# State injection of an S5 layer with the tokens as the stationary operand, and moved modulation panels

## The chip, the cores and the metric

The kernel runs on one core of a Trainium2 chip. The metric is the device time of one execution in microseconds (us). Before: 2250.16 us, the median of three runs (2249.39 to 2253.13).

## The reference, cut to what matters

Four layers on 256 latent and 256 context tokens of 1024 channels: attention, Hyena, S5, FNet, each followed by a SwiGLU feed-forward (FFN). The change lies in the S5 mixer (layer 2), in the join ahead of it and in the one ahead of FNet (layer 3). S5 computes, for both directions, a linear recurrence over the context tokens and then over the latent ones:

```
bu = einsum('bngc,gsc->bngs', u, b_bar)        # the injection: 64 groups of 16 channels, 64 complex states each
xs = associative_scan(_lin_rec, (lam_bar, bu), reverse=reverse)
xs_lat = xs_lat + a_cum * h0                    # the context's last state carried into the latent tokens
y_lat = y_lat + einsum('bngs,gcs->bngc', xs_lat, c_mat).real
out = a * sigmoid(b), a, b = split(gelu(y_lat) @ w_glu + b_glu)
```

At FNet: `f = fftn(hg, axes=(1, 3)).real`, then a projection; the transform over channels comes first.

## The kernel before, in words

Every engine runs its own hand-written list of work, stage by stage, and semaphores order them. The program's classes are stages: `Join` (the norm, residual and modulation between two sub-layers), `S5`, `Ffn`, `Fnet`. Eight steps of tokens form a chunk, so a direction has 32 context and 32 latent chunks of 8 tokens; the scan runs over chunks, the inside of a chunk is done by a Toeplitz product.

**S5 on TensorE** (`S5.tensor`). The injection runs 16 rounds of four groups. Each round has eight matmuls (L2470) with a 128 x 128 block of weights `et` as the stationary operand and 64 columns of tokens `u` (32 latent and 32 context chunks) as the moving one; their sum lies in bank 0 or 1 with the states on the partitions, forward states on partitions 0 to 63, backward ones on 64 to 127. In the trace an ordinary f32 matmul stands as two MATMUL records, a transpose as one. After round 7 TensorE takes the "turn" of one modulation unit (L374). Then come 64 Toeplitz matmuls (L2484), two modulation panels ("states", L397), the first half of the output products (L2497), four panels ("scan"), the second half, the transposes of y (L2508) with two panels ("turns") between, and the gated projection `up` (L864).

**ScalarE** (`S5.scalar`) moves each round's bank to `e` with three copies (helper line L2516), which put the states in the order of the scan: `e` is (group, real or imaginary, step q in a block of 8 chunks, block b), context ahead of latent blocks, backward rows reversed. **VectorE** (`S5.vector`) first lays out tables (until L2361), waits for `e_moved` and scans: `inside` (L2370 to L2373, seven steps of four operations), `across` (L2380 to L2383), for groups 0 to 15, 16 to 31, then 32 to 63, and at last `carries` (L2425 to L2428) of the second half. GpSimd does the `carries` of the first half once `across` of it is done. ScalarE and VectorE then copy the states to `s2` for the output products.

**SyncE** issues the DMAs in one written order: `et` blocks 0 to 3, the power table, two modulation panels, half of the `u` tokens (GpSimd issues the other half), two modulation panels, eight Toeplitz blocks `m0`, `et` blocks 4 to 7 as slots come free, the output weights `f` in two halves, then modulation panels and the weights of `up`. `f` lies over `et` and `m0`.

**Modulation** (`Modulations`). The 24 vectors that modulate the layers are products with 96 panels of 1 MB. `place(key, n, before)` gives n panels to a slot of TensorE's order and says when SyncE may refetch the two ring buffers. Four panels make a unit; ScalarE copies a finished unit (L408), TensorE turns it (L374), VectorE adds the bias (L418 and the next two). In `Join.tensor` part 0 stands ahead of the spreads (L495), part 1 behind them. `build` gives the join ahead of S5 (2, 2) panels and the join ahead of FNet (2, 0). That last one has a turn in part 1 and nothing else. By this count panels 82 and 83 are part 1 ahead of S5, 84 and 85 "states", 86 to 89 "scan", 90 and 91 "turns".

**FNet** (`Fnet.tensor`): 16 matmuls over channels (L2590), copied by VectorE (L2609), then 32 over tokens (L2599), then the projection (L819). L2590 needs only the channel blocks of h that it reads, which ScalarE writes one by one (L693).

## Time and profile before

| | us |
|---|---|
| median of three runs | 2250.16 |
| the profiled execution | 2252.99 |
| its span in the profile | 2251.2 |
| TensorE busy | 2106.3 (94%) |
| VectorE busy | 1167.2 (52%) |
| ScalarE busy | 865.4 (38%) |
| GpSimd busy | 156.0 (7%) |

Busy is the time in which an engine had an instruction under way; a TensorE that is busy need not stream columns at its full rate. PEclk is the granted clock of TensorE as a share of 2.4 GHz: 1.00 is 2.4 and 0.50 is 1.2 GHz. Idle time is followed by what ended it. "Bank" is PSUM, "arena", "ring" and "tail" are areas of SBUF. Times in rows are us from the start of the span.

### The profile page before, as it was taken

The numbers are of one execution on the slowest core, as the hardware profiler recorded it, in microseconds if no ns is written. First come the engines' busy times: TensorE is split into PE (matmuls) and PEld (weight loads), VectorE is DVE, ScalarE is ACT, GpSimd is POOL, SyncE is SP. The second block draws the span as 40 slices with busy tenths as digits, with TensorE's granted clock in tenths as the row PEclk, the third lists the DMA queues.
The fourth block names the chain that finished last, engine by engine and source line by source line (L and its number), as shares of the span: only waits on it lengthen the run. The fifth ranks groups of instructions, "written<-read, shape, count | busy, mean of one in ns | idle before, by whom it ended". The sixth has DMA issues, their size and how long they took to land.

```text
span 2251.2 us, 31615 instructions
## 1 busy us (share of the span) xinstructions
PE 2106.3 (94%) x13233; PEld 1650.2 (73%) x13233; DVE 1167.2 (52%) x1961; ACT 865.4 (38%) x1416; POOL 156.0 (7%) x213
## 2 busy tenths in 40 slices
PE   4999999999999989988999999997959899898998
PEld 2756557777777767754558888884948899778997
DVE  2322652655566566636254665765571645526454
ACT  2442224533333453220243334245632544525444
POOL 0000000102001100010001200111110000000000
PEclk8999999999999999999999999998579999999998
DMA  6334341645435546442143433444584555314553
GB/s 255 131 124 168 131 149 38 197 146 169 175 133 190 174 150 226 165 144 75 38 150 120 129 117 115 136 138 159 206 337 138 181 187 187 125 57 150 188 180 102
DMA packets 227243, 342.14 MB, mean 152 GB/s; under 512 B 9590, under 2 KB 190625, under 8 KB 224860
## 3 DMA queue, kind: packets, MB, share of 16 engines
q1 hardware_dynamic: 216064, 310.27, 40.2%
q0 software_dynamic: 10320, 29.58, 4.5%
q8 instruction: 105, 1.72, 0.3%
q10 hardware_dynamic: 716, 0.26, 0.0%
q14 instruction: 38, 0.31, 0.0%
HBM read 317.66 MB, written 24.51 MB: 152 GB/s over the span
## 4 chain that ended last, share of the span: by engine, by line
PE 86%; DVE 7%; DMA 3%; ACT 2%; issue 1%; SPq 0%; POOL 0%; ACTq 0%; DVEq 0%
PE bank L953 20%; PE bank L954 20%; PE bank L955 20%; PE bank L819 4%; PE bank L397 4%; PE bank L864 2%; PE bank L2470 2%; PE bank L1719 1%; DMA mod_ring<-mod_w 1%; PE bank L1348 1%; PE bank L637 1%; DMA arena<-mod_w 1%; PE bank L2052 1%; PE bank L627 1%; PE bank L495 1%; PE bank L1673 1%
## 5 line engine op out<-in xcount | busy, mean ns | idle before, releaser
L953 PE MATMUL bank<-h_hi,w_hi 128*128 128x512 f32 (+1 forms) x1480 | 512.4, 346 | 11.1 <-DVE h_lo L725 10.6
L954 PE MATMUL bank<-h_lo,w_hi 128*128 128x512 f32 (+1 forms) x1480 | 505.0, 341 | 0.0
L955 PE MATMUL bank<-h_hi,w_lo 128*128 128x512 f32 (+1 forms) x1480 | 505.0, 341 | 0.0
L915 DVE TENSOR_TENSOR w_lo<-ring,w_hi 128x1024 fp32r<-128x1024 f32 (+1 forms) x282 | 323.8, 1185 | 285.0 <-ACT w_hi L910 284.9
L953 PEld LDWEIGHTS bank<-h_hi,w_hi 128*128 128x128 f32 x1480 | 283.6, 192 | 49.5 <-DVE h_lo L725 13.3
L910 ACT ACTIVATE w_hi<-ring 128x1024 fp32r<-128x1024 f32 (+1 forms) x282 | 274.0, 1019 | 103.8 <-PE bank L955 100.8
L955 PEld LDWEIGHTS bank<-h_hi,w_lo 128*128 128x128 f32 x1480 | 283.4, 191 | 32.1 <-issue 0.2
L954 PEld LDWEIGHTS bank<-h_lo,w_hi 128*128 128x128 f32 x1480 | 283.8, 192 | 29.3 <-issue 0.2
L953 PE MATMUL bank<-g_hi,w_hi 128*128 128x512 f32 (+1 forms) x704 | 241.1, 342 | 0.0
L954 PE MATMUL bank<-g_lo,w_hi 128*128 128x512 f32 (+1 forms) x704 | 236.9, 337 | 0.0
L955 PE MATMUL bank<-g_hi,w_lo 128*128 128x512 f32 (+1 forms) x704 | 236.7, 336 | 0.0
L953 PEld LDWEIGHTS bank<-g_hi,w_hi 128*128 128x128 f32 x704 | 133.5, 190 | 22.6 <-issue 8.7
L955 PEld LDWEIGHTS bank<-g_hi,w_lo 128*128 128x128 f32 x704 | 133.5, 190 | 14.3
L954 PEld LDWEIGHTS bank<-g_lo,w_hi 128*128 128x128 f32 x704 | 133.6, 190 | 12.9
L1073 ACT ACTIVATE g_hi<-arena 128x512 fp32r<-128x512 f32 (+1 forms) x88 | 45.9, 525 | 234.6 <-DVE arena L1098 234.6
L397 PE MATMUL bank<-mod_ring,silu_c 128*32 128x256 f32 x1408 | 98.6, 406 | 24.6 <-DMA mod_ring<-mod_w 24.6
L1067 ACT ACTIVATE arena<-bank 128x512 f32<-128x512 f32 (+1 forms) x88 | 42.7, 490 | 189.4 <-PE bank L955 187.8
L1098 DVE TENSOR_TENSOR arena<-arena,bank 128x512 f32<-128x512 f32 (+1 forms) x88 | 48.2, 551 | 112.6 <-PE bank L955 110.6
L397 PEld LDWEIGHTS bank<-mod_ring,silu_c 128*32 128x32 f32 x1408 | 40.4, 114 | 66.5 <-DMA mod_ring<-mod_w 31.1
L953 PE MATMUL bank<-h_hi,hy_w_hi 128*128 128x512 f32 x192 | 76.5, 398 | 0.7 <-DVE h_lo L725 0.7
L954 PE MATMUL bank<-h_lo,hy_w_hi 128*128 128x512 f32 x192 | 74.9, 390 | 0.0
L955 PE MATMUL bank<-h_hi,hy_w_lo 128*128 128x512 f32 x192 | 74.8, 390 | 0.0
(328 smaller groups left out, 2978.3 us busy)
## 6 DMA issues: line engine op xcount, KB each, us to landing
ring<-ffn_w SPq DMA_DIRECT2D x120, 1024.0 KB, 5.1
mod_ring<-mod_w SPq DMA_DIRECT2D x88, 1024.0 KB, 6.8
ring<-ffn_w SPq DMA_DIRECT2D x16, 768.0 KB, 4.6
ring<-hy_w_in SPq DMA_DIRECT2D x12, 1024.0 KB, 5.2
arena<-mod_w SPq DMA_DIRECT2D x8, 1024.0 KB, 17.1
s_in_weights<-arena POOLq DMA_DIRECT2D x32, 256.0 KB, 3.2
s_out_weights<-arena POOLq DMA_DIRECT2D x16, 512.0 KB, 3.6
arena<-s_in_weights SPq DMA_DIRECT2D x8, 1024.0 KB, 10.8
```

The costliest lines, as they stand in the source:

```text
L397: last = nc.tensor.matmul(MODB[32 * g:32 * g + 32, 0:256], silu_c[:, k, :], self.slot(m)[:, kk, 256 * g:256 * g + 256], start=(k == 0), st ...
L819: last = nc.tensor.matmul(self.banks[c % 4][:, 0:self.n], v[:, kl, q * P:(q + 1) * P], self.rhs(k), start=(k == 0), stop=(k == self.kk - 1))
L864: last = nc.tensor.matmul(self.bank(c, t)[:, 0:self.n], v[:, k, q * P:(q + 1) * P], self.rhs(k), start=(k == 0), stop=(k == KD - 1))
L910: nc.scalar.activation(self.hi[:, i % SPLIT, a:b], self.w.slot(i)[:, a:b], ACT.Copy).then_inc(w_rounded, 1)
L915: unit.tensor_tensor(self.lo[:, i % SPLIT, a:b], self.w.slot(i)[:, a:b], self.hi[:, i % SPLIT, a:b].bitcast(F32), ALU.subtract).then_inc(w ...
L953: nc.tensor.matmul(o, w[0], v[0], start=first, stop=False)
L954: nc.tensor.matmul(o, w[0], v[1], start=False, stop=False)
L955: return nc.tensor.matmul(o, w[1], v[0], start=False, stop=last)
L1067: nc.scalar.activation(self.silus[:, q, 0:n], self.out(i, q)[:, 0:n], ACT.Silu).then_inc(ffn_silu, 1)
L1073: nc.scalar.activation(g_hi[:, c + q, 0:n], self.silus[:, q, 0:n], ACT.Copy).then_inc(ffn_g_rounded, 1)
L1098: nc.vector.tensor_tensor(self.silus[:, q, 0:n], self.silus[:, q, 0:n], self.out(i, q)[:, 0:n], ALU.mult).then_inc(ffn_product, 1)
L2470: last = nc.tensor.matmul(bank[self.INJECT[n % 2]][:, o:o + 2 * CH], self.et[:, c % 4, 4 * (n % 2) + gb, i, :], self.u[:, 4 * n + gb, :], ...
```

## The change

The injection swaps its operands. In each round the 64 token columns of a group are the stationary operand and the 256 weights (128 real, 128 imaginary states) the moving one; four matmuls write bank 0 or 1, two groups side by side on partitions 0 to 63 and 64 to 127, tokens on the partitions (`inject`). The bank is copied to `rows` in SBUF, by VectorE for rounds 0 to 3 and by ScalarE for 4 to 15 (`move_injected`). Eight small products then bring the states back to the partitions (`turn_states`): four transposes for the forward states, four matmuls with the identity read backwards within each 32 columns for the backward ones. They write bank 4 or 5 directly in the order of `e`, in steps of eight elements, and ScalarE copies the bank with one plain copy. The latent and context halves of `h_split` change places. TensorE's order is inject(0), inject(1), turn_states(0), inject(2), turn_states(1) and so on.

GpSimd's carries wait for all rounds, as `rows` lies where they work. The Toeplitz products run in plain order and wait for `e_moved` before their second half. SyncE issues `et` 4 to 7 right behind the tokens, and the modulation fetches later. Panels 82 and 83 move from the join to "states", whose four panels follow the Toeplitz products; the turn that stood behind round 7 is now in "states" too, and VectorE takes it between the two halves of its scan. The last turn moves from the join ahead of FNet to between FNet's two transforms.

```diff
@@ Join @@
             def place_mods(self, counts=(2, 2), before=None):
-                self.fills = True
+                self.fills = len(counts)
...
-                if self.fills:
+                if self.fills == 2:
                     mods.tensor(pe, (self, 1))
...
-                            dst = h_split[:, :, k, a // LAT, :].rearrange("p s m -> p m s")
+                            dst = h_split[:, :, k, 1 - a // LAT, :].rearrange("p s m -> p m s")
@@ S5.gpsimd @@
                 for qt in range(4):
                     self.tokens(pool, 1, qt)
+                pool.wait_ge(self.e_moved, self.NB)
                 pool.wait_ge(self.step, self.SCAN[0])
@@ S5.__init__ @@
+                self.rows = self.t0.rearrange("p (a n) -> p a n", a=2)
...
-                mods.place((self, "turn"), 0)
-                mods.place((self, "states"), 2, p0 + 0.3)
+                mods.place((self, "states"), 4, p0 + 0.3)
@@ S5.sync @@
                     if c >= 4:
-                        sp.wait_ge(self.e_summed, 2 * (c - 4) + 2)
+                        sp.wait_ge(self.e_summed, self.injected(2 * (c - 4) + 1))
...
-                mods.refill(sp, p0 + 0.1)
                 for qt in range(4):
                     self.tokens(sp, 0, qt)
+                for c in range(4, 8):
+                    inject(c)
                 mods.refill(sp, p0 + 0.2)
...
                 for c in range(8):
                     toeplitz(c)
-                for c in range(4, 8):
-                    inject(c)
-                sp.wait_ge(self.e_summed, self.NB)
+                sp.wait_ge(self.e_summed, self.injected(self.NB - 1))
                 for hf in range(2):
                     if hf:
                         sp.wait_ge(self.m_summed, 1)
+                        mods.refill(sp, p0 + 0.3)
                     for c in range(4 * hf, 4 * hf + 4):
@@ S5.vector @@
                 dve.wait_ge(self.placed, 16)
+                for n in range(4):
+                    self.move_injected(dve, V.tensor_copy, n)
...
                     for gs in self.PARTS[hf]:
-                        dve.wait_ge(self.e_moved, 3 * gs.stop // 4)
+                        dve.wait_ge(self.e_moved, gs.stop // 4)
                         inside(gs)
-                        if gs.start == 0:
-                            mods.vector(dve, (self, "turn"))
                     across(slice(32 * hf, 32 * hf + 32))
+                    if hf == 0:
+                        mods.vector(dve, (self, "states"))
...
-                for key in ("states", "scan", "turns"):
+                for key in ("scan", "turns"):
@@ S5, new functions @@
+            def injected(self, n):
+                return 2 * n if n else 1
+            def turned(self, n):
+                return min(2 * n + 3, 2 * self.NB)
+            def inject(self, pe, n):
+                c = n // 2
...
+                if n >= 2:
+                    pe.wait_ge(self.placed, 16 + n - 1)
+                for p in range(2):
+                    for z in range(2):
+                        gb = 2 * p + z
+                        last = nc.tensor.matmul(bank[self.INJECT[n % 2]][64 * z:64 * z + 64, 256 * p:256 * p + 256], self.u[:, 4 * n + gb, :],
+                                                self.et[:, c % 4, 4 * (n % 2) + gb].rearrange("p i n -> p (i n)"), start=True, stop=True)
+                last.then_inc(self.e_summed, 1)
+            def move_injected(self, eng, copy, n):
+                eng.wait_ge(self.e_summed, self.injected(n))
+                if n >= 2:
+                    eng.wait_ge(self.e_summed, self.turned(n - 2))
+                copy(self.rows[:, n % 2], bank[self.INJECT[n % 2]][:, :]).then_inc(self.placed, 1)
+            def turn_states(self, pe, n):
+                pe.wait_ge(self.placed, 16 + n + 1)
+                if n >= 2:
+                    pe.wait_ge(self.e_moved, n - 1)
+                dst = bank[self.STATES[n % 2]][:, :].rearrange("p (a z i q b) -> p a i z b q", a=2, z=2, i=2, q=BLK)
+                back = ident[:, :].rearrange("p (a t) -> p a t", t=CH)[:, :, ::-1]
+                for p in range(2):
+                    for i in range(2):
+                        src = self.rows[:, n % 2, 256 * p + P * i:256 * p + P * i + P]
+                        nc.tensor.transpose(dst[0:STATE, p, i], src[:, 0:STATE], ident[:, :])
+                        last = nc.tensor.matmul(dst[STATE:P, p, i], src[:, STATE:P], back, start=True, stop=True)
+                last.then_inc(self.e_summed, 1)
@@ S5.tensor @@
-                for n in range(self.NB):
...
-                    if n >= 2:
-                        pe.wait_ge(self.e_moved, 3 * (n - 1))
-                    for gb in range(4):
-                        for i in range(2):
-                            o = (2 * gb + i) * 2 * CH
-                            last = nc.tensor.matmul(bank[self.INJECT[n % 2]][:, o:o + 2 * CH], self.et[:, c % 4, 4 * (n % 2) + gb, i, :], self.u[:, 4 * n + gb, :],
-                                                    start=True, stop=True)
-                    last.then_inc(self.e_summed, 1)
-                    if n == 7:
-                        mods.tensor(pe, (self, "turn"))
+                for n in range(self.NB + 1):
+                    if n < self.NB:
+                        self.inject(pe, n)
+                    if n:
+                        self.turn_states(pe, n - 1)
                 pe.wait_ge(self.m_loaded, 16 * (1 + 8))
...
-                for idx in (*range(8, 16), *range(8)):
+                for idx in range(16):
                     hf, gl = divmod(idx, 8)
-                    if idx == 0:
-                        pe.wait_ge(self.e_moved, 3 * self.NB)
+                    if idx == 8:
+                        pe.wait_ge(self.e_moved, self.NB)
@@ S5.scalar @@
                 for n in range(self.NB):
-                    act.wait_ge(self.e_summed, n + 1)
-                    src = bank[self.INJECT[n % 2]][:, :].rearrange("p (g b q) -> p g b q", g=8, q=BLK)
-                    dst = self.e[:, 4 * n:4 * n + 4].rearrange("p g r q b -> p (g r) b q")
-                    copy(dst[0:STATE, :, 4:8], src[0:STATE, :, 0:4]).then_inc(self.e_moved, 1)
-                    copy(dst[0:STATE, :, 0:4], src[0:STATE, :, 4:8]).then_inc(self.e_moved, 1)
-                    copy(dst[STATE:P, :, ::-1, ::-1], src[STATE:P]).then_inc(self.e_moved, 1)
+                    if n >= 4:
+                        if n == 4:
+                            act.wait_ge(self.placed, 16 + 4)
+                        self.move_injected(act, copy, n)
+                    act.wait_ge(self.e_summed, self.turned(n))
+                    copy(self.e[:, 4 * n:4 * n + 4].rearrange("p g r q b -> p (g r q b)"), bank[self.STATES[n % 2]][:, :]).then_inc(self.e_moved, 1)
+                mods.scalar(act, (self, "states"))
                 act.wait_ge(self.carried, 8)
@@ Fnet @@
+                mods.place((self, "turn"), 0)
...
                         last.then_inc(self.chan, 1)
+                mods.tensor(pe, (self, "turn"))
                 for g2 in range(KD // 2):
                     pe.wait_ge(self.chan_moved, 5 + g2)
...
                     nc.vector.tensor_copy(self.a[...], bank[n % 4][:, :]).then_inc(self.chan_moved, 1)
+                mods.vector(dve, (self, "turn"))
@@ build @@
             if l == 1:
-                post.place_mods((2, 2), (len(panels) + 0.1, len(panels) + 0.2))
+                post.place_mods((2, 0), (len(panels) + 0.2, None))
             if l == 2:
-                post.place_mods((2, 0))
+                post.place_mods((2,))
```

## Rows read from the trace of the kernel before

**Rows 1.** The chain that ended last, 1540 to 1760: start us, us, what.

```profile
1566.73 9.51 DMA arena<-h_sb
1576.29 27.57 PE bank L2470 x128
...
1633.92 0.70 DVE bank L2370
...
1669.43 3.82 ACT tail L2516 x2
1673.34 5.29 PE bank L2497 x128
```

**Rows 2.** Line 2470 and its durations in ns (minimum/median/maximum).

```profile
L2470 PEld LDWEIGHTS bank<-arena x256: 288/333/338, 1576.3 to 1631.0; 128*128 128x128 f32 x128
L2470 PE MATMUL bank<-arena x256: 314/421/472, 1576.3 to 1631.1; 128*128 128x64 f32 x128
```

**Rows 3.** Stretches: us, busy (x instructions) per engine, PEclk, DMA share, GB/s.

```profile
1552.00:1563.00 11.00, 5.47 (x72) 3.63 (x72) 8.34 (x16) 4.04 (x8) 0.00 (x0) 1.00 0.98 391
1590.00:1604.00 14.00, 14.00 (x67) 14.00 (x68) 10.74 (x27) 9.05 (x13) 0.00 (x0) 0.50 1.03 417
1632.00:1635.00 3.00, 3.00 (x64) 2.78 (x60) 1.08 (x2) 1.79 (x3) 2.84 (x3) 0.50 0.82 281
1636.00:1639.00 3.00, 2.91 (x76) 1.85 (x68) 2.90 (x5) 0.00 (x0) 3.00 (x2) 1.00 1.02 423
```

**Rows 4.** TensorE in order of time: start us, us, what, xcount [idle before <-releaser].

```profile
1631.42 5.76 PE L2484 MATMUL bank<-arena 128*32 128x128 f32 x128
1637.01 1.90 PE L397 MATMUL bank<-mod_ring,silu_c 128*32 128x256 f32 x32
...
1657.55 1.07 PE L397 MATMUL bank<-mod_ring,silu_c 128*32 128x256 f32 x16 [0.22 <-DMA mod_ring<-mod_w]
...
1667.41 1.94 PE L397 MATMUL bank<-mod_ring,silu_c 128*32 128x256 f32 x16 [1.57 <-DMA mod_ring<-mod_w]
...
1678.56 1.09 PE L2508 MATMUL bank<-ident,arena 128*128 128x128 f32 x8
```

**Rows 5.** ScalarE and VectorE in order of time around the scan.

```profile
1673.15 1.05 ACT L2516 ACTIVATE arena<-bank 128x512 f32<-128x512 f32 x2
...
1575.59 0.22 DVE L2361 TENSOR_SCALAR bank<-ring 128x64 f32<-128x64 f32 x1
...
1604.59 0.17 DVE L418 TENSOR_TENSOR modv<-bank,vec 128x16 f32<-128x16 f32 x1
...
1606.19 0.43 DVE L2370 TENSOR_TENSOR bank<-bank,arena 128x256 f32<-128x256 f32 x1 [1.01 <-ACT arena L2516]
...
1618.15 0.27 DVE L2380 TENSOR_TENSOR bank<-bank,arena 128x64 f32<-128x64 f32 x1
```

**Rows 6.** GpSimd and the DMA issues of SyncE around the scan.

```profile
1625.42 2.32 POOL L2425 TENSOR_TENSOR ring<-ring,arena 128x896 f32<-128x896 f32 x1 [45.84 <-DVE arena L2383]
...
1641.30 2.08 POOL L2428 TENSOR_TENSOR arena<-arena,ring 128x896 f32<-128x896 f32 x1
...
1582.91 4.10 SPq L2314 DMA_DIRECT2D arena<-s_toeplitz  x8
```

**Rows 7.** The start of the FNet layer, 1960 to 1985, three engines.

```profile
1965.10 0.60 ACT L693 ACTIVATE h_sb<-arena,modv,affine 128x256 f32<-128x256 f32 x1 [2.98 <-DVE arena L721]
...
1971.35 0.42 DVE L721 TENSOR_TENSOR arena<-x_sb,bank 128x256 f32<-128x256 f32 x1
...
1975.16 0.69 DVE L2609 COPY arena<-bank 128x512 f32<-128x512 f32 x1 [1.32 <-PE bank L2590]
...
1972.73 0.69 PE L374 MATMUL bank<-ident,mod_rows 128*128 128x128 f32 x2 [8.19 <-ACT mod_rows L408]
1973.21 8.96 PE L2590 MATMUL bank<-arena,h_sb 128*128 128x256 f32 x32
1982.01 13.98 PE L2599 MATMUL bank<-arena 128*128 128x256 f32 x64
```

More of the change, by code:

```diff
@@ L550, in __init__ @@
                 self.rows = n // 4
-                self.first, self.fills = None, False
+                self.first, self.fills = None, 0
                 self.sq = Tally(y_squared, KD)
@@ L700, in scalar @@
                 if self.fills:
-                    for part in range(2):
+                    for part in range(self.fills):
                         mods.scalar(act, (self, part))
@@ L776, in vector @@
                 if self.fills:
-                    for part in range(2):
+                    for part in range(self.fills):
                         mods.vector(dve, (self, part))
@@ L2406, in vector @@
                             src = bank[self.TURNED[hf][z]][:, :].rearrange("p (s j m) -> p s j m", s=4, j=4)[:, :, j, :]
-                            V.scalar_tensor_tensor(self.yk[:, k, 4 * z:4 * z + 4], h_split[:, 4 * z:4 * z + 4, k, 0, :], vcol("s5_d", k), src,
+                            V.scalar_tensor_tensor(self.yk[:, k, 4 * z:4 * z + 4], h_split[:, 4 * z:4 * z + 4, k, 1, :], vcol("s5_d", k), src,
                                                    ALU.mult, ALU.add).then_inc(self.skipped, 1)
@@ L2447, in backward @@
                 copy(dst[:, :, ::-1, BLK - 2::-1], src[:, :, 4:8, 0:BLK - 1]).then_inc(done, 1)
-            INJECT, OUT, TURNED = (0, 1), (0, 1, 4, 5), ((0, 1), (4, 5))
+            INJECT, STATES, OUT, TURNED = (0, 1), (4, 5), (0, 1, 4, 5), ((0, 1), (4, 5))
             def collect(self, copy, b, done):
@@ L2455, in collect @@
                 copy(self.ysb[:, hf, :, gl:gl + 4, :], bank[self.OUT[b]][:, :].rearrange("p (g s c) -> p s g c", g=4, c=GC)).then_inc(done, 1)
-            def tensor(self, pe):
-                for n in range(self.NB):
-                    c = n // 2
-                    if n % 4 == 0:
-                        for e in range(2):
-                            pe.wait_ge(self.u_loaded[e][n // 4 % 2], 16 * 4 * (n // 8 + 1))
-                    if n % 2 == 0:
-                        pe.wait_ge(self.w_loaded[c % 4], 16 * (c // 4 + 1))
-                    if n >= 2:
-                        pe.wait_ge(self.e_moved, 3 * (n - 1))
-                    for gb in range(4):
-                        for i in range(2):
-                            o = (2 * gb + i) * 2 * CH
-                            last = nc.tensor.matmul(bank[self.INJECT[n % 2]][:, o:o + 2 * CH], self.et[:, c % 4, 4 * (n % 2) + gb, i, :], self.u[:, 4 * n + gb, :],
-                                                    start=True, stop=True)
-                    last.then_inc(self.e_summed, 1)
-                    if n == 7:
-                        mods.tensor(pe, (self, "turn"))
+            def injected(self, n):
+                return 2 * n if n else 1
@@ new lines, in turned @@
+            def turned(self, n):
+                return min(2 * n + 3, 2 * self.NB)
+            def inject(self, pe, n):
+                c = n // 2
+                if n % 4 == 0:
+                    for e in range(2):
+                        pe.wait_ge(self.u_loaded[e][n // 4 % 2], 16 * 4 * (n // 8 + 1))
+                if n % 2 == 0:
+                    pe.wait_ge(self.w_loaded[c % 4], 16 * (c // 4 + 1))
+                if n >= 2:
[6 more added lines that the diff above has]
+                last.then_inc(self.e_summed, 1)
@@ L2478, in out @@
                     return bank[self.OUT[idx // 4]][32 * j:32 * j + 32, (idx % 4) * P:(idx % 4 + 1) * P]
-                for idx in (*range(8, 16), *range(8)):
+                for idx in range(16):
                     hf, gl = divmod(idx, 8)
-                    if idx == 0:
-                        pe.wait_ge(self.e_moved, 3 * self.NB)
+                    if idx == 8:
+                        pe.wait_ge(self.e_moved, self.NB)
                     for j in range(4):
-                        last = nc.tensor.matmul(out(idx, j), self.u[:, self.place(hf, gl, j), 0:CH], self.m0[:, 8 * (4 * hf + j) + gl, :],
+                        last = nc.tensor.matmul(out(idx, j), self.u[:, self.place(hf, gl, j), CH:2 * CH], self.m0[:, 8 * (4 * hf + j) + gl, :],
                                                 start=(idx % 4 == 0), stop=False)
@@ L2527, in scalar @@
                 self.backward(act, copy, 0, self.s_moved)
-                for key in ("turn", "states", "scan"):
-                    mods.scalar(act, (self, key))
+                mods.scalar(act, (self, "scan"))
                 act.wait_ge(self.step, sum(self.SCAN))
```

## The prediction

> **What bounds the kernel now.** I read the chain of waits first, for the stretch that the change touches. From 1566.7 to 1678.6 us it runs through a DMA of tokens, then 55 us of L2470 on TensorE, the scan of the second half on VectorE (1633.92 to 1669.43), a copy on ScalarE and the output products [rows 1]. So the S5 mixer is serial: injection, second half of the scan, output. Next the records of L2470: 128 matmuls, two records each, with a weight load of 128 columns for every 64 moving columns [rows 2]. From 1576.3 to the first Toeplitz product at 1631.42 [rows 4] that is 55.1 us, 3.44 a round. TensorE counts as busy all that time, yet its granted clock is 0.50, that is 1.2 GHz [rows 3]. The Toeplitz products behind it run denser, and within them the clock rises to 1.00, between 3.6 and 4.6 us after their start [rows 3, 4]. ScalarE's three copies a round hide under the matmuls, and VectorE waits for rounds.
>
> **Prices.** A stream of 256 columns: 32 such matmuls take 13.98 us at the full clock [rows 7], 0.43 each with two records. Column groups side by side cost nothing extra: two panels of 16 matmuls, four abreast, take 1.90 us, one panel 1.07, so the second adds 0.83, and about 0.24 is filling and draining [rows 4]. At 1.2 GHz a panel takes 1.94 [rows 4].
>
> **Injection.** Removed are eight weight-load-bound matmuls a round (3.44 us). Added are `inject`, two rounds of two 256-column matmuls abreast, 2 x 0.43 = 0.86 us at full clock, and `turn_states`, four rounds of a 128-column matmul with a transpose beside it, 4 x 0.215 = 0.86 us. At half clock each is 1.72, together 3.44: exactly what is there now. No row shows two 64-wide column groups, a backward-read moving operand, or a PSUM output in steps of eight. Bounds: below, nothing extra, as for the four 32-wide groups; above, no overlap at all: inject 1.72, turn 4 x (0.215 + 0.11) = 1.3 us at full clock, where 0.11 is less than 1.09/8 for a transpose [rows 4], its drain taken off. I take full overlap, since the panels of the same kernel show it for 32-wide groups.
>
> The Trainium skill's page "PSUM — Partial Sum Buffer", section "Specifications (TRN2)", says that any non-contiguous access pattern slows matmuls significantly. It speaks against this change, as all eight products of a turn write in steps of eight. No row here has such an output. If it holds, that is rival 1 below.
>
> **The clock.** The new work streams columns all the time while TensorE is the bound, as the Toeplitz products do, and not half the time. I take the rise after 4.3 us, as there. Later gaps should not bring it down: between 1552 and 1563 TensorE was busy 5.5 of 11 us, in short pieces, and kept 1.00 [rows 3].
>
> **First rounds.** VectorE is free at 1575.8 [rows 5]; before that it can move nothing. Its copy of 128x512 out of PSUM is 0.69 [rows 7], so turn 0 starts near 1576.6. inject 0 and 1 lie before that, as the tokens land earlier: the DMA wait of 9.51 us [rows 1] stood behind two panels of 1 MB, at 391 GB/s [rows 3] about 5 us, which are now fetched later. Should they not come earlier, it costs about 1.5 us. Up to turn 3 there are three injects and four turns: 7 x 0.86 = 6.0, plus 2.15 for 4.3 us at half clock, plus 0.3 and ScalarE's copy of 0.6: `e_moved` reaches 4 at about 1585.7.
>
> **Later rounds.** ScalarE now has two copies of 0.52 (1.05 for two [rows 5]), in this order: copy of round n, which waits for turn n, then move of n+1, for which turn n+1 waits. That loop is 0.86 turn + 0.24 drain + 1.05 + 0.15 of handoffs = 2.3 us, longer than TensorE's own 1.72. So ScalarE becomes the bound: the 16th round is moved at 1585.7 + 12 x 2.3 = 1613.3, TensorE is done at 1612.6.
>
> **VectorE.** A part of 16 groups takes 1618.15 - 1606.19 = 11.96 us, `across` until GpSimd starts 7.27 [rows 5, 6]: 1585.7 + 31.2 = 1616.9. Then comes the added wait: `mods.vector("states")` stands ahead of the second half and needs the turn, and the turn needs Toeplitz (64 matmuls, 3.5 at full clock), two panels (1.90), ScalarE's copy and the transposes (about 1.0): 1612.6 + 6.4 = 1619.0, plus 0.6 for VectorE's three small operations (1604.59 to 1605.2 [rows 5]). The second half starts at 1619.7 and not 1633.92: 14.2 us gained. Everything of it waits behind that turn; every 0.1 us on a later round costs 1.2 us.
>
> **SyncE and GpSimd.** SyncE waits for inject 7 (about 1590) before the last `et` block, then two panels and 4 MB of Toeplitz blocks, which it took 4.10 us to issue [rows 6]: 7 MB at 417 GB/s [rows 3] land near 1608, 4 us ahead of need. `f`'s second half is now queued behind four refills, the last of which waits for panel 85 (about 1625): it lands near 1640, needed near 1659. GpSimd's new wait (16 rounds, 1613) ends before the old one (1617); it starts 8.4 us earlier. The first output half follows to about 1649. The four "scan" panels took 1669.35 - 1657.55 = 11.8 us behind it [rows 4], of which waiting for the first two goes: about 10, so 1659. The second output half starts at 1659.3 against 1673.34 [rows 1]: 14.0 gained. VectorE's second half alone would allow 1659.1, so the panels are next in line. The two more panels of "states" stand where TensorE had nothing to do.
>
> **FNet.** Now the turn waits 8.19 us for ScalarE, which copies the unit only after all of h, and the transforms stand behind it [rows 7]. After: the first four groups of L2590 run while h is written (from 1965.7 [rows 7]); VectorE is free at 1971.8, its copies of 0.69 and four more groups alternate, 0.86 each, to 1976.1 [rows 7]; the turn 0.4. L2599 starts at 1976.5 and not 1982.01: 5.5 us gained. Even at half clock throughout, 16 matmuls x 0.86 from 1965.8 end at 1979.6: at least 2 us.
>
> **Sum.** 14.0 + 5.5 = 19.5. The profiled execution of 2252.99 (span 2251.2) would be 2233.5; the median of 2250.16 lies 2.8 lower, so 2230.7: I say 2231.
>
> **Rivals.** *1, slower turns.* Without overlap of the transposes a turn is 1.3, a round 2.75: the second half starts 4 x 0.44 + 12 x 0.44 = 7 us later, 2238. With writes at half rate a turn is 1.72: 16 x 0.86 = 13.8 later, 2245. For it: no row of such an output; against it: f32 columns come at only 256 in 0.43 us. 17%. *2, the clock stays at 1.2 GHz.* Then rounds are 3.44 and packed: `e_moved` 4 at 1589.5, TensorE done at 1630.0; Toeplitz 5.8, panels 1.9, turn 1.6: the second half starts at 1639.3, 5.4 later than now, and FNet gives it back: 2250. For it: L2470 stayed there for 55 us. 10%. *3, slower than before.* Half clock and no overlap between neighbours, at the same place. If only the transposes run alone, a round is 4.3, 16 x 0.87 = 14 us more: 2264; if nothing overlaps, 6.0 a round, 2290. It decides from about 3.75 us a round. 6%. *4, a late transfer:* Toeplitz blocks or the panels in front of the output arrive 3 to 10 us late, 2237 to 2245. 7%. That the moved turn does nothing: the wait of 8.19 us in FNet speaks against it [rows 7].
>
> **How the numbers follow.** The forecast has 60%, with 2226 to 2237 as its own range: a round 0.2 longer costs 2.4, tokens no earlier 1.5, FNet 3; the other way the output products at full clock give 1.5 and earlier panels 2. Range over all: 2226 to 2248, which leaves out most of rivals 2 and 3. A measurement of this kernel can tell about 0.2%, 4.5 us, from no change. Faster: 60 + 16 + 7 + 1 = 84%; same: 1 + 8 = 9%; slower: 7%.
>
> **What would show it.** In the new profile: a clock of 1.00 from about 1581; turns of 0.9 us and 2.3 us a round; ScalarE nearly full in rounds 4 to 15; VectorE idle some 2.5 us before the second half, ended by L374; L2599 at 5.5 us less behind the last L693. Wrong would be: rounds of 3.4 or more, a clock of 0.50, or TensorE waiting for a DMA before Toeplitz or the second output half.

## The result and the profile after

| | before | after |
|---|---|---|
| median of 6 runs each | 2249.99 us | 2257.82 us |
| lowest to highest | 2249.39 to 2253.13 | 2256.43 to 2259.34 |
| profiled execution (span) | 2252.99 (2251.2) | 2259.34 (2257.5) |

The ratio after to before is 1.0029, 95% interval 1.0018 to 1.0039. The kernel got slower by about 0.3%. The forecast was 2231 with 2226 to 2248: wrong, and in the sign too.

From the page of after, span and busy time of each engine:

```profile
span 2257.5 us, 31757 instructions
...
PE 2106.4 (93%) x13297; PEld 1622.8 (72%) x13297; DVE 1171.2 (52%) x1965; ACT 845.2 (37%) x1396; POOL 156.5 (7%) x213
```

**Where in the span.** Executions differ by up to 6 us in what lies ahead of the S5 mixer: the reciprocal of `r_pre` in front of it starts anywhere between 1555.15 and 1561.02 in the twelve traces of this study. I therefore count from that reciprocal (1558.57 before, 1560.94 after). The second half of the scan starts 75.35 us behind it before and 87.02 after; the second output half 114.77 before and 126.45 after. S5 lost 11.7 us where 14 were to be gained. FNet gained: its transforms no longer wait for the turn.

TensorE of after in order of time (start us, us, engine line operation, shapes, count, idle before and what ended it): the first injects, the first turn, the Toeplitz products and the second output half. L2534 is what L2497 was [rows 1, 4].

```profile
1573.24 3.28 PE L2481 MATMUL bank<-arena 128*64 128x256 f32 x16 [9.54 <-DMA arena<-h_sb]
1579.60 0.42 PE L2502 MATMUL bank<-ident,ring 128*64 128x128 f32 x1 [3.08 <-DVE ring L2489]
...
1638.04 5.04 PE L2521 MATMUL bank<-arena 128*32 128x128 f32 x128
...
1687.39 5.94 PE L2534 MATMUL bank<-arena,tail 128*32 128x128 f32 x128 [6.78 <-ACT tail L2553]
```

The same view in FNet, against [rows 7]:

```profile
1988.65 0.38 PE L374 MATMUL bank<-ident,mod_rows 128*128 128x128 f32 x2
1988.87 13.98 PE L2638 MATMUL bank<-arena 128*128 128x256 f32 x64
```

The turn (L374) has no wait in front of it, where it had 8.19 us, and L2638 follows at once. The second transform starts 4.40 us behind the start of the last L694 (1988.87 against 1984.47), where before it started 10.20 us behind the last L693 (1982.01 against 1971.81): 5.8 us gained.

**The clock rose.** Stretches of after: busy time of each engine, then the granted clock, DMA share and GB/s.

```profile
1585.00:1586.00 1.00, 1.00 (x4) 0.42 (x3) 0.69 (x1) 0.00 (x0) 0.00 (x0) 0.50 0.38 156
1586.00:1587.00 1.00, 1.00 (x7) 0.43 (x5) 0.00 (x0) 0.00 (x0) 0.00 (x0) 0.89 0.08 33
1590.00:1634.00 44.00, 40.56 (x247) 21.00 (x246) 29.07 (x84) 12.54 (x23) 0.00 (x0) 1.00 0.59 223
...
1638.00:1640.00 2.00, 2.00 (x41) 1.82 (x44) 0.00 (x0) 0.60 (x1) 1.17 (x1) 0.50 1.01 426
```

Between 1586 and 1587 it goes from 0.50 to 1.00 and stays through all rounds, with TensorE busy for 40.56 of 44 us. It falls within the last turn: the mean is 0.71 from 1637 to 1638, behind two stretches in which TensorE had gaps (busy 0.24 us from 1634 to 1635 and 0.58 us from 1635 to 1636, both still at 1.00). In the Toeplitz products it is at 0.50 from 1638 to 1640 and back at 1.00 from 1641 on.

**The turn is what went wrong.** One round of after at the full clock: TensorE from the turn of one round to that of the next, then ScalarE's copy of the round (`arena`) and move of the next one (`ring`). L2502 is the transpose, L2503 the product of the same block with the backward-read identity, L2481 `inject`.

```profile
1599.28 0.30 PE L2502 MATMUL bank<-ident,ring 128*64 128x128 f32 x1 [0.31 <-ACT ring L2553]
1599.51 0.43 PE L2503 MATMUL bank<-ident,ring 128*64 128x128 f32 x2
1599.87 0.30 PE L2502 MATMUL bank<-ident,ring 128*64 128x128 f32 x1
1600.10 0.43 PE L2503 MATMUL bank<-ident,ring 128*64 128x128 f32 x2
1600.46 0.30 PE L2502 MATMUL bank<-ident,ring 128*64 128x128 f32 x1
...
1601.06 0.30 PE L2502 MATMUL bank<-ident,ring 128*64 128x128 f32 x1
...
1601.45 0.27 PE L2503 MATMUL bank<-ident,ring 128*64 128x128 f32 x1
1601.56 1.03 PE L2481 MATMUL bank<-arena 128*64 128x256 f32 x7
1602.90 0.30 PE L2502 MATMUL bank<-ident,ring 128*64 128x128 f32 x1 [0.31 <-ACT ring L2553]
...
1601.76 0.60 ACT L2553 ACTIVATE arena<-bank 128x512 f32<-128x512 f32 x1 [2.53 <-PE bank L2503]
1602.25 0.59 ACT L2553 ACTIVATE ring<-bank 128x512 f32<-128x512 f32 x1
```

A turn is four times L2502 and L2503. The pairs start 0.59 us apart (1599.28, 1599.87, 1600.46, 1601.06), and the last product ends at 1601.45 + 0.27 = 1601.72: the turn lasts 2.4 us. I had 0.86. Inject behind it is as forecast, and so are ScalarE's two copies, 1.1 us together. The round is 1602.90 - 1599.28 = 3.62 us; over the nine rounds from 1599.28 to 1631.81 it is 3.61, against 2.3 forecast and 3.44 before.

**The added wait.** VectorE of after around the start of the second half (same columns):

```profile
1645.86 0.17 DVE L418 TENSOR_TENSOR modv<-bank,vec 128x16 f32<-128x16 f32 x1 [16.97 <-PE bank L374]
1646.07 1.76 DVE L425 SCALAR_TENSOR_TENSOR affine<-modv,vec 128x16 f32<-128x16 f32 x1
...
1647.96 0.69 DVE L2374 TENSOR_TENSOR bank<-bank,arena 128x512 f32<-128x512 f32 x1
```

It waited 16.97 us for L374's turn, which stands behind all rounds, the Toeplitz products and two panels, where the old kernel had its three small operations done early.

### The profile page after: what moved, and what is told of

It is laid out like the page before. It is cut to its first block, busy times and chain, and to the rows that moved or that the text cites. A ratio compares the mean times of both kernels' runs of the same rounds, so it can differ in the third digit from the quotient of the medians.

```text
span 2257.5 us, 31757 instructions
## 1 busy us (share of the span) xinstructions
PE 2106.4 (93%) x13297; PEld 1622.8 (72%) x13297; DVE 1171.2 (52%) x1965; ACT 845.2 (37%) x1396; POOL 156.5 (7%) x213
## 4 chain that ended last, share of the span: by engine, by line
PE 86%; DVE 7%; DMA 3%; ACT 2%; issue 1%; SPq 0%; POOL 0%; ACTq 0%; DVEq 0%
PE bank L954 21%; PE bank L955 20%; PE bank L956 20%; PE bank L820 4%; PE bank L397 4%; PE bank L865 2%; PE bank L1720 1%; DMA mod_ring<-mod_w 1%; PE bank L2503 1%; PE bank L1349 1%; PE bank L637 1%; DMA arena<-mod_w 1%; PE bank L2053 1%; PE bank L627 1%; PE bank L1674 1%
## 5 line engine op out<-in xcount | busy, mean ns | idle before, releaser
L397 PE MATMUL bank<-mod_ring,silu_c 128*32 128x256 f32 x1408 | 97.3, 402 | 17.9 <-DMA mod_ring<-mod_w 17.9
L397 PEld LDWEIGHTS bank<-mod_ring,silu_c 128*32 128x32 f32 x1408 | 40.2, 112 | 58.5 <-DMA mod_ring<-mod_w 23.7
```

What stands on the lines that cost most here:

```text
L397: last = nc.tensor.matmul(MODB[32 * g:32 * g + 32, 0:256], silu_c[:, k, :], self.slot(m)[:, kk, 256 * g:256 * g + 256], start=(k == 0), st ...
```

## The experiments

All counts from the reciprocal, in us, each from one profiled execution; "second half" is the first L2374 on 128x512 behind `across`, "second output" the second L2534. Times are medians. The ratio is that of the kernel to the kernel before on the same chip, whose medians were 2249.55 to 2251.85 there.

| kernel | round | second half | second output | time | ratio (95%) |
|---|---|---|---|---|---|
| before | 3.44 | 75.35 | 114.77 | 2249.99 | 1 |
| after | 3.61 | 87.02 | 126.45 | 2257.82 | 1.0029 (1.0018 to 1.0039) |
| t_contig | 3.61 | 85.41 | 124.82 | 2251.94 | one run |
| v_later | 3.61 | 77.27 | 119.69 | 2251.82 | 1.0003 (0.9993 to 1.0013) |
| t_grouped | 2.82 | 72.36 | 111.80 | 2245.44 | one run |
| t_matmul | 2.28 | 63.58 | 103.02 | 2235.34 | one run |
| one_mode | 2.28 | 61.11 | 100.52 | 2229.18 | 0.9913 (0.9890 to 0.9936) |
| full_plain | 1.83 | 62.74 | 102.17 | 2235.01 | one run |
| both | 2.28 | 56.42 | 100.12 | 2231.22 | 0.9916 (0.9900 to 0.9933) |
| both_six | 2.28 | 58.86 | 98.78 | 2228.02 | 0.9899 (0.9879 to 0.9918) |
| panels_back | 2.28 | 63.05 | 102.48 | 2232.56 | 0.9916 (0.9893 to 0.9939) |
| f_only | 3.44 | 75.11 | 114.51 | 2243.95 | 0.9974 (0.9964 to 0.9983) |

Theories on the turn: **A**, a stepped PSUM output is slow; **B**, a transpose and an ordinary product don't run side by side and each change of kind costs time; **C**, the backward-read moving operand is slow.

### t_contig: the outputs of a turn contiguous

```diff
-                dst = bank[self.STATES[n % 2]][:, :].rearrange("p (a z i q b) -> p a i z b q", a=2, z=2, i=2, q=BLK)
+                dst = bank[self.STATES[n % 2]][:, :].rearrange("p (a i n) -> p a i n", a=2, i=2)
```

> The changed kernel, but the eight products of a turn write 128 neighbouring elements each instead of elements in steps of eight, so the states stand in the wrong order and the output is not the reference's. A turn takes 2.37 us at the full clock in the changed kernel. Theory A (the strided PSUM output slows the products): a turn falls to about 1.3 us and a round from 3.61 to about 2.6 us, the whole to about 2240. Theory B (the neighbours do not overlap and every switch between a transpose and an ordinary product costs time): the turn stays at 2.3 to 2.4 us and the whole at 2257.

This kernel leaves out the scan's order: the states stand in PSUM as they come, all else is as in after. TensorE of t_contig, one round:

```profile
1602.79 0.30 PE L2502 MATMUL bank<-ident,ring 128*64 128x128 f32 x1 [0.31 <-ACT ring L2553]
...
1603.38 0.30 PE L2502 MATMUL bank<-ident,ring 128*64 128x128 f32 x1
...
1606.41 0.30 PE L2502 MATMUL bank<-ident,ring 128*64 128x128 f32 x1 [0.31 <-ACT ring L2553]
```

The pairs still start 0.59 us apart, the round is 1606.41 - 1602.79 = 3.62 us here too. A falls: the stepped output costs nothing here. The run's time below after's is no part of this: its reciprocal is 5.5 us earlier (1555.46 against 1560.94), ahead of the changed place, and the second half 1.6 (85.41 against 87.02). All of these 1.6 lie ahead of the Toeplitz products, which start at 75.50 instead of 77.10 with the same later rounds: the clock is at 1.00 for part of the first turn and rises for good at about 1578.5, 23 us behind the reciprocal, where in after it is 25.

### t_matmul and one_mode: the transpose as an ordinary product

```diff
-                        nc.tensor.transpose(dst[0:STATE, p, i], src[:, 0:STATE], ident[:, :])
+                        nc.tensor.matmul(dst[0:STATE, p, i], src[:, 0:STATE], ident[:, :], start=True, stop=True)
```

> The changed kernel with ordinary products against the identity in place of the four transposes of a turn: 16 records instead of 12, all of one kind. Theory A (strided output): no gain, a turn gets longer, to 2.5 us or more, since four more records write in steps of eight. Theory B (switching between the transpose and the ordinary mode): the turn falls to 1.0 to 1.3 us although it has more records, a round to 2.4 to 2.6, the whole to about 2240.

The same kernel again, with more rounds of timing, as one_mode:

> The same kernel as t_matmul (ordinary products against the identity for the four transposes), now timed against the kernel before. One look gave 2235.3. Theory (the forecast was right but for the price of the switches): 14 to 20 us less than before, 2231 to 2237. Rival (the one look stood on a favourable start of the S5 layer): under 10 us less.

TensorE of one_mode: first and last of the eight steps of a turn, inject, and the next turn:

```profile
1601.21 0.32 PE L2502 MATMUL bank<-ident,ring 128*64 128x128 f32 x1 [0.32 <-ACT ring L2553]
1601.22 0.32 PE L2503 MATMUL bank<-ident,ring 128*64 128x128 f32 x1
...
1602.03 0.27 PE L2502 MATMUL bank<-ident,ring 128*64 128x128 f32 x1
1602.04 0.27 PE L2503 MATMUL bank<-ident,ring 128*64 128x128 f32 x1
1602.14 1.03 PE L2481 MATMUL bank<-arena 128*64 128x256 f32 x8
1603.49 0.32 PE L2502 MATMUL bank<-ident,ring 128*64 128x128 f32 x1 [0.32 <-ACT ring L2553]
```

L2502 and L2503 now start 0.01 us apart, in eight steps of 0.11 us, 1601.21 to 1602.04: a turn takes 0.9 us though the transposing product has two records where the transpose had one. Outputs are stepped and L2503 still reads the identity backward, so C falls as well. The round is 2.28 us; the time is 19.6 us below before by the ratio's 0.9913. Further on in one_mode:

```profile
1606.80 3.70 PE L2521 MATMUL bank<-arena 128*32 128x128 f32 x128
...
1652.72 1.93 PE L397 MATMUL bank<-mod_ring,silu_c 128*32 128x256 f32 x16 [0.54 <-DMA mod_ring<-mod_w]
1655.67 4.65 PE L2534 MATMUL bank<-arena,tail 128*32 128x128 f32 x84 [1.01 <-issue]
```

The Toeplitz products keep the full clock, 3.70 us against 5.04 in after. The last panel ends at 1654.65. What the second output half waits for behind it is ScalarE's copy of the states, which runs from 1651.72 to 1655.57; the row names no releaser. So the scan sets its start here, with the panels 1.0 us behind.

### t_grouped: four transposes, then four products

```diff
                for p in range(2):
                    for i in range(2):
                        src = self.rows[:, n % 2, 256 * p + P * i:256 * p + P * i + P]
                        nc.tensor.transpose(dst[0:STATE, p, i], src[:, 0:STATE], ident[:, :])
+                for p in range(2):
+                    for i in range(2):
+                        src = self.rows[:, n % 2, 256 * p + P * i:256 * p + P * i + P]
                        last = nc.tensor.matmul(dst[STATE:P, p, i], src[:, STATE:P], back, start=True, stop=True)
```

> The changed kernel with the four transposes of a turn first and the four ordinary products behind them, nothing else: two switches between the kinds in a turn in place of eight. Theory (each switch has a price, the records themselves take 0.11 us each and overlap only with their own kind): a turn falls from 2.37 us to between 1.0 and 1.6, a round to 2.4 to 2.8, the whole to 2235 to 2242. Rival (each transpose into 64 partitions is slow by itself): a turn stays above 2 us.

```profile
1602.17 0.63 PE L2502 MATMUL bank<-ident,ring 128*64 128x128 f32 x4 [0.31 <-ACT ring L2556]
1602.73 0.76 PE L2506 MATMUL bank<-ident,ring 128*64 128x128 f32 x5
...
1604.99 0.63 PE L2502 MATMUL bank<-ident,ring 128*64 128x128 f32 x4 [0.31 <-ACT ring L2556]
```

The first product starts 1602.73 - 1602.17 = 0.56 us behind the first transpose; with one change of kind in it that is some 0.11 a transpose. The round is 1604.99 - 1602.17 = 2.82 us. Nothing but the order differs from after, where a round has eight changes of kind (with inject) and here two: (3.61 - 2.82) / 6 = 0.13 us for one. Between 2.82 and the 2.28 of one_mode lies what remains: two changes, 0.26, and four transposes of 0.11, which stand ahead of the products instead of running abreast; that makes 0.70, of which 0.54 is seen. Both halves of B can be read in after, too: a product starts 0.23 us behind its transpose and the next transpose 0.36 us behind the product (1599.28, 1599.51, 1599.87), where the instructions themselves take 0.11 and 0.215. So they don't run abreast, and each change adds 0.12 to 0.15 us.

### full_plain: the whole turn as four transposes of 128 columns

```diff
-                        nc.tensor.transpose(dst[0:STATE, p, i], src[:, 0:STATE], ident[:, :])
-                        last = nc.tensor.matmul(dst[STATE:P, p, i], src[:, STATE:P], back, start=True, stop=True)
+                        last = nc.tensor.transpose(dst[:, p, i], src, ident[:, :])
```

> The changed kernel with four transposes of 128 columns in place of the eight products, all writing in steps of eight; the backward states then stand in forward order, so the output is not the reference's. Theory A (strided output costs about twice the time of a record): a transpose takes about 0.25 us from start to start and the turn 1.0. Theory B (only switching costs): 0.11 to 0.13 us as for y's transposes, the turn 0.5. In both the round is about 2.0 to 2.5 us, now bound by ScalarE's loop, and the whole about 2235.

This kernel leaves out the reversal: backward states stand in forward order. The round falls to 1.83 us, and the second half starts no earlier than in one_mode (62.74 against 61.11). TensorE and then VectorE of full_plain:

```profile
1612.04 6.30 PE L2519 MATMUL bank<-arena 128*32 128x128 f32 x128 [4.10 <-DMA arena<-s_toeplitz]
...
1621.12 0.17 DVE L418 TENSOR_TENSOR modv<-bank,vec 128x16 f32<-128x16 f32 x1 [3.24 <-PE bank L374]
```

The rounds no longer set the end. TensorE waits 4.10 us for the Toeplitz blocks, takes 6.30 us for their products (the clock is 0.50 from 1612 to 1616), and VectorE still waits 3.24 us for the turn behind them. So with faster rounds the transfer of the Toeplitz blocks is next in line, which is the forecast's rival 4.

### v_later: the added wait behind the inner steps of the second half

```diff
+                        if hf:
+                            mods.vector(dve, (self, "states"))
...
-                    if hf == 0:
-                        mods.vector(dve, (self, "states"))
```

> The changed kernel with VectorE's part of the moved turn behind the inner steps of its second half instead of ahead of that half; nothing else moves. In the changed kernel VectorE stood idle 16.97 us until the turn and began the second half at 1647.96, though the last round was moved at 1638.8. Theory (the turn is what is late): it begins near 1639, 9 us earlier, and the whole is 9 us less, about 2249. Rival (the output half on TensorE waits for panels or for GpSimd anyway): under 3 us gained.

VectorE and then TensorE of v_later:

```profile
1636.49 0.70 DVE L2374 TENSOR_TENSOR bank<-bank,arena 128x512 f32<-128x512 f32 x1 [10.54 <-ACT arena L2553]
...
1677.20 1.94 PE L397 MATMUL bank<-mod_ring,silu_c 128*32 128x256 f32 x16 [0.53 <-DMA mod_ring<-mod_w]
1678.91 4.86 PE L2534 MATMUL bank<-arena,tail 128*32 128x128 f32 x128
```

The second half waits for ScalarE's last move, no longer for L374, and starts at 77.27 instead of 87.02. The second output gains 6.8 of these 9.8 us, since the last panel (1677.20) now stands in front of it. About 0.6 us of both gains is not the edit's: the Toeplitz products start at 76.47 here and at 77.10 in after. So some 6 us of after's loss came through this wait, which the medians agree with (2251.82 against 2257.82).

The 4.9 us that the second output still lies over before come through the other wait that the change added, GpSimd's for all rounds. GpSimd of v_later:

```profile
1636.47 2.35 POOL L2429 TENSOR_TENSOR ring<-ring,arena 128x896 f32<-128x896 f32 x1 [58.17 <-ACT arena L2553]
```

Its carries start with ScalarE's last move, 77.25 us behind the reciprocal, where before they started at 66.85 [rows 6]. The first output half follows 10.4 us later than before (103.09 against 92.68), and the panels in front of the second output half stand behind it. The chain that ended last runs through exactly these. Without it ScalarE's copy of the second half's states, done at 1676.30, would have let the second output start at about 117.2, 2.4 over before. The forecast let GpSimd's wait end early, at 1613, on rounds of 2.3 us.

### f_only: the kernel before with the FNet part alone

```diff
+                mods.place((self, "turn"), 0)
...
+                mods.tensor(pe, (self, "turn"))
...
+                mods.vector(dve, (self, "turn"))
...
-                post.place_mods((2, 0))
+                post.place_mods((2,))
```

> The kernel before with the last turn moved from the join to between FNet's two transforms, and nothing else of the change. By the prediction 5.5 us less than before, about 2244.5, with the second transform 5.5 us earlier behind the last modulation. Rival (the clock falls in the longer trickle of the first transform, or VectorE's copies set the pace): 2 us or less.

0.9974 of before, 5.8 us (3.8 to 8.1 by the interval); forecast 5.5. Only the join ahead of FNet and FNet are changed. L374 starts at 1973.77 without a wait and the transforms behind it at 1973.98, as in after: 4.39 us behind the start of the last L693 (1969.59) and not 10.20 as before.

### both, both_six and panels_back: what is next in line

```diff
# both: one_mode and v_later together; both_six also:
-                mods.place((self, "states"), 4, p0 + 0.3)
-                mods.place((self, "scan"), 4, p0 + 0.4)
+                mods.place((self, "states"), 6, p0 + 0.3)
+                mods.place((self, "scan"), 2, p0 + 0.4)
# panels_back: one_mode, with the two late panels fetched and used early again:
-                mods.place((self, "states"), 4, p0 + 0.3)
+                mods.place((self, "states"), 2, p0 + 0.3)
+                mods.refill(sp, p0 + 0.1)
-                post.place_mods((2, 0), (len(panels) + 0.2, None))
+                post.place_mods((2, 2), (len(panels) + 0.1, len(panels) + 0.2))
```

> t_matmul with VectorE's part of the moved turn behind the inner steps of its second half. Theory A (VectorE's wait and its three small operations are what is late): the second half starts 4.6 us earlier and the whole is 4 us less than t_matmul. Theory B (the panels in front of the second output half are next in line; they were read until 1662.1 and ScalarE's copy ended at 1662.8): under 1.5 us less than t_matmul.

> The kernel of both with six panels in front of the first output half and two behind it, in place of four and four; the second half of the output weights is then issued behind six refills. In both, the second output half started at 1660.05 when the last panel in front of it had been read, while the states for it were ready some 4 us earlier. Theory (those panels are next in line): with two panels there, fetched during the 13 us in which TensorE waits for the first states, the second output half starts 3 to 4 us earlier and the whole is 3 us less than both, about 2228. Rival (the weights of the gated projection, or the output weights behind six refills, come too late): no gain or a loss of 1 to 5 us.

> one_mode with panels 82 and 83 back in the join and two panels in states, fetched as in the kernel before; the turn stays in states. Theory A (the panels' move buys the earlier tokens, about 1.5 us, and takes 1.9 us of panels away from the chain that VectorE waits for, which hardly counts): 0 to 2 us more than one_mode, 2230. Theory B (the token DMAs wait again behind 2 MB of panels and the injection starts 3 to 5 us later): 3 to 6 us more, 2233 to 2236.

In both the second half starts 4.7 us earlier than in one_mode (56.42 against 61.11), and the second output 0.4: the gain goes into the panels in front of it, as named in the forecast. both_six takes two of the four away. TensorE of both_six, from the first output half to the second:

```profile
1642.09 6.01 PE L2534 MATMUL bank<-arena,tail 128*32 128x128 f32 x128 [8.16 <-ACT tail L2553]
1648.04 0.44 PE L374 MATMUL bank<-ident,mod_rows 128*128 128x128 f32 x2
1648.40 1.93 PE L397 MATMUL bank<-mod_ring,silu_c 128*32 128x256 f32 x32
1654.34 5.04 PE L2534 MATMUL bank<-arena,tail 128*32 128x128 f32 x128 [4.00 <-ACT tail L2553]
```

Behind the first output half only one batch of panels is left (L397, no wait), and the second half waits 4.00 us for ScalarE. Against both, the second output is 1.3 us earlier in the traces, though its second half starts 2.4 us later, as the clock of its first rounds was at 0.50 until about 1578.6 and that of both at 1.00; the ratios, 0.9899 and 0.9916, differ by 3.8 us, but their intervals overlap. both_six is the best version run: 22.7 us below before. panels_back shows what the two late panels alone are worth: second output at 102.48 instead of 100.52 in one trace each, no difference by the ratios (0.9916 and 0.9913). Its first inject starts 17.5 us behind the reciprocal instead of 11.8, its first turn 20.0 instead of 18.1, since VectorE, which has to move the first round, becomes free at the same place in both.

## Why the prediction was wrong

**The step that failed is "Injection", the term of `turn_states`.** It had 4 x 0.215 = 0.86 us, with 1.3 as its upper bound. It measured 2.4. The bound added the transpose's own time to the product's and had no price for going from one kind to the other; the rows of before held no place where a transpose and an ordinary product alternate, so "no overlap at all" looked like the worst case. What is there: eight changes of 0.13 us make 1.04, four transposes of 0.11 make 0.44, four products of 0.215 make 0.86, together 2.3 of the 2.4 measured. I took overlap from panels of four column groups, which are all of one kind; one_mode shows that rule to hold for two groups of one kind.

**What it made of the start of the second half**, term by term, 1647.96 against 1619.7, 28.3 us late:

| term | late by |
|---|---|
| execution ahead of S5 (reciprocal 1560.94 against 1558.57) | 2.4 |
| first turn 1579.60 against 1576.6, less the 2.4 | 0.6 |
| first four turns, 4 x 1.5, and 0.4 more | 6.4 |
| twelve rounds of 3.61 instead of 2.3 | 15.7 |
| last round | 0.3 |
| Toeplitz 5.04 instead of 3.5 (clock back at 0.50) | 1.4 |
| VectorE's small operations 2.1 instead of 0.6 | 1.5 |

22.4 of the 28.3 are the turn, the last round's 0.3 among them. Its first 6.4 also hold a later rise of the clock, which came 6.5 us behind the first turn instead of 4.3; these rows don't part the two. The Toeplitz term goes along with it: the products took 5.04, 4.73 and 4.29 us in after, t_contig and v_later, whose turns alternate, and 3.70 in t_grouped, t_matmul and one_mode. Why the clock fell there is not shown.

**What held.** The clock rose, though at 1586 to 1587 and not about 1581. ScalarE's loop does bound the round once the turn is right: 2.28 against 2.3. VectorE's added wait was placed rightly, behind Toeplitz and panels, and costs what the rounds put into it. The panels are next in line behind it. The Toeplitz blocks came in time in after, though not for the faster rounds of full_plain. FNet gave 5.8 for 5.5. And the sum holds for one_mode, which differs from after by one operation: 19.6 us (14 to 25 by the interval) for 19.5.

Part of that agreement is luck. The second half of one_mode starts at 61.11, and the forecast's 1619.7 is 61.1 too, but two errors cancel. The Toeplitz products start at 51.65, where the forecast's 1612.6 is 54.0: the clock was at 1.00 from 1573 on, when the first turn began, so the 2.15 us for a half clock did not come. Behind them 9.5 us pass instead of 7.1, since VectorE's three small operations took 3.0 us instead of 0.6. t_matmul is the same kernel in an execution whose clock was 0.50 until past 1582; its second half starts at 63.58.

**The rivals.** Rival 1 named slower turns, with two causes: no overlap (2238), which was half of the truth, and PSUM writes at half rate (2245), which t_contig refutes. The Trainium skill's page "PSUM — Partial Sum Buffer", section "Specifications (TRN2)", says that a non-contiguous access pattern slows matmuls significantly; for f32 outputs in steps of eight the rounds of 3.61 us with and without the step don't agree with it. Rivals 2 and 4 did not occur in after; a late transfer shows only in full_plain. Rival 3 had the right sign. Of its two conditions, half clock and no overlap between neighbours, only the second came, and the loss came at the full clock. Its point of 3.75 us a round was also too high. FNet gives 5.8 us back, so the kernels are level where S5 loses no more than that: after's 11.7 us at 3.61 must come down by 5.9, over 16 rounds 0.37 each, which puts the point near 3.25 us a round. t_grouped at 2.82 agrees with that, with a second output 3.0 us earlier than before's.

The Trainium skill's page "Perfetto Trace Analysis", section "Transposes", advises to write a logical transpose as a transpose and not as a standard matmul. Here the runs say the opposite: beside ordinary products the matmul form is 1.5 us a turn faster. Its page "TensorEngine Tiling (Array Packing)", section "Gotcha 2: Feature Incompatibilities", lists the transpose mode with f32 input as excluded with column tiling. That fits the missing overlap; the runs do not show it to be the reason, and no page there gives the price of a change.

## What to carry to other kernels

A cost taken from rows of one kind of instruction says nothing about two kinds in turn: where a change alternates them, look for a row of the alternation, and if there is none, put a price on each change of kind in the upper bound and measure it first. If a small transpose has to stand between ordinary products, write it as a product with the identity, or group the transposes. And a wait added in front of the critical engine turns every delay of what it waits for into time; put it behind the work that has slack. An engine off the chain can be brought onto it by such a wait, as GpSimd was in v_later.

## What the runs showed of the hardware

**A change between transpose and ordinary product costs 0.13 us on TensorE** (f32, 64 by 128 columns, full clock), and neighbours of different kinds don't overlap, while two column groups of 64 of the same kind do so fully: 0.11 us a step for two records.

**A stepped f32 PSUM output is free**: 3.61 us a round with steps of eight and without; in one_mode all eight products of a turn write in steps of eight at 0.11 us a step.

**Small operations of VectorE can be held by GpSimd.** VectorE, then GpSimd, of one_mode:

```profile
1613.48 0.58 DVE L425 SCALAR_TENSOR_TENSOR affine<-modv,vec 128x16 f32<-128x16 f32 x1
1614.10 2.23 DVE L429 TENSOR_TENSOR affine<-affine,vec 128x16 f32<-128x16 f32 x1
...
1613.99 2.31 POOL L2430 TENSOR_TENSOR ring<-ring,arena 128x896 f32<-128x896 f32 x1
```

L429 on 128x16 usually takes 0.17 us. Here it takes 2.23, 1614.10 to 1616.33, and GpSimd's L2430 ends at 1616.30. In after it is L425 that is held, from 1646.07 to 1647.83, and this row of GpSimd ends at 1647.81:

```profile
1645.73 2.08 POOL L2432 TENSOR_TENSOR arena<-arena,ring 128x896 f32<-128x896 f32 x1
```

Neighbours with an operand in PSUM (L418, L2374) kept their 0.17 and 0.69 us. The Trainium skill's page "SBUF — State Buffer", section "Who interferes with whom", says that a VectorE instruction with two SBUF inputs contends with a GpSimd instruction that reads SBUF, and the loser blocks until the other is done; the rows agree. It is the 1.5 us of the table's last line. No run was made for this, but those on record part the two cases. In the five other runs in which these operations stand beside GpSimd's products (t_contig, t_matmul, t_grouped, full_plain, panels_back) L425, L429 or both are held the same way. In panels_back it is both, and GpSimd's rows end at 1619.65 and 1621.92:

```profile
1617.42 2.25 DVE L425 SCALAR_TENSOR_TENSOR affine<-modv,vec 128x16 f32<-128x16 f32 x1
1619.71 2.24 DVE L429 TENSOR_TENSOR affine<-affine,vec 128x16 f32<-128x16 f32 x1
```

In before, v_later, both, both_six and f_only GpSimd is idle when they run, and each takes 0.17 or 0.18 us.
